# The value projection of both attention layers by the seven-product scheme

## The chip, the cores and the metric

One Trainium2 chip, one core of it. The metric is the device time of one execution in microseconds (us), the median of several runs. The program is one launch; all arithmetic is f32.

## The reference, cut to what matters

256 tokens of width 1024 pass through four layers, then through two more of another kind. Layers 0 and 3 of the first four are forgetting attention, with their own weights (j = 0 and j = 1 below):

```
h = rms_norm(x, mix_norm_g[i])
proj = h @ w_in                       # w_in 1024 x 3088
q, k, v, f_logit = split(proj, [1024, 2048, 3072])
log_f = log_sigmoid(f_logit + b_f);  c = cumsum(log_f)
p = softmax(q k^T / 8 + c_q - c_k, causal);  out = (p @ v) @ w_out
```

The change concerns `v = h @ w_in[:, 2048:3072]`, a product of 256x1024 by 1024x1024. The norm's division by the token's root mean square is a scaling of rows and is done after the product; the norm's weights are multiplied into the transposed tokens before.

## The kernel before, in words

The five engines each have one program; they meet at semaphores. Weights stream from HBM through `ring`, three slots of 128 x 6144 f32. The SyncE program issues every weight load in the order of use, three transfers per slot (line 504), each adding 16 to `loaded[slot]`; TensorE takes a slot when the count is 48 (`take`, line 1021), and gives it back with the first matmul after its last use (`release` and `carry`, lines 1048 to 1055). SyncE waits for that before it loads the slot again. For an attention layer the pieces are, in order: columns 2560 to 3087 of w_in (the right half of v and the 16 forget gates), columns 2048 to 2559 (the left half of v), four pieces of q and k, two of w_out (`fox`, line 526). The GpSimd queue loads the parameters of the S5 layer in the first microseconds (line 993), much of it in runs of 64 bytes.

The attention layer, TensorE's side (`fox`, line 1293): `raw_xT` turns the tokens, 16 transposes into banks 0 to 3; VectorE multiplies them by the norm's weights into `xT` (line 1979). Then 8 matmuls give the forget gates in bank 7 (line 1071), one matmul with a diagonal of the token scales gives these scales along columns in bank 6 (`scale_cols`, line 1129), and in layer 3 one transpose turns the norm vectors of later layers (line 1302, bank 0). The value projection is 32 matmuls of line 1082: for each half of the columns and each half of the tokens, 8 slices of the inner dimension, 128x128 by 128x512. Each bank is read by VectorE in one scaling (line 2203), into `v_rows`. After it `project(0)` (line 1316) makes the first pair of heads' q and k in bank 7, 16 matmuls; in layer 0 the transposes of `s5_inputs` follow (line 1382), and then attention, pair after pair, with `project(i + 1)` ahead of pair i.

VectorE's side (`fox`, line 2187) is one fixed order: the four xT copies, the reciprocal and diagonal of the token scales (2045, 2047), the copy of the scales (2052), forget gates (2193, 2195), in layer 3 the copy to `norm_vec` (2199), the four value scalings, the cumulative sum of the gates (2206 to 2211), in layer 0 the sign changes of S5 parameters (2263 to 2265), then the q and k scalings.

The seven-product scheme is already in use in the FFN layers: `token_sums` (line 1989) makes four sums of token blocks, `weight_sums` (2001) and `down_sums` (2015) make three new weight sums and overwrite one block, TensorE makes seven products of half the inner dimension (lines 1178 and 1230) in place of eight, and VectorE adds them up (`add_products`, line 2138). `then` (1955) has VectorE wait for its own operation before the next.

Of the kernel before, what the change touches and what calls it, by code (L numbers as in the profile page):

```python
# [10 lines left out]
S = 256  # L11
# [183 lines left out]
def build(nc, inp, table, out):  # L195
# [3 lines left out]
    with ctx:  # L199
# [87 lines left out]
        S1, S2, S3, S4 = (s_sum[:, i] for i in range(4))  # L287
        xA = [[xT[:, 4 * h:4 * h + 4, i * P:(i + 1) * P] for h in range(2)] for i in range(TT)]
# [132 lines left out]
        prods_read = sem("products_read")  # L421
        FAST_USE = [8]
# [593 lines left out]
        def _(pe):  # L1016
# [276 lines left out]
            def fox(j):  # L1293
# [658 lines left out]
        def _(dve):  # L1952
# [22 lines left out]
            def raw_xT(g, banks, sums=True):  # L1975
                for j, b in enumerate(banks):
# [5 lines left out]
                    if sums and j == 1:  # L1982
                        dve.wait_ge(drained_dve, t.value("drained_dve"))
                        token_sums(early=True)
                if sums:
                    dve.wait_ge(drained_dve, t.value("drained_dve"))
                    token_sums(early=False)

            def token_sums(early):

                (a11, a12), (a21, a22) = xA
                tt = dve.tensor_tensor
# [194 lines left out]
            def fox(j):  # L2187
                raw_xT(VEC_AT["mix_norm_g"] + 3 * j * KD, (0, 1, 2, 3), sums=False)
                scale_diag()
                full()  # L2190
                scale_cols(6)
# [4 lines left out]
                   .then_inc(dve_to_act, 1)  # L2196
                if j == 1:
# [658 lines left out]
```

## Time and profile before

| | |
|---|---|
| median of 3 runs | 2743.18 us (2739.14, 2743.18, 2746.19) |
| profiled execution, its own time | 2741.28 us |
| its span in the trace | 2739.4 us, 83867 instructions |
| TensorE matmul busy | 2651.6 us, 97% |
| TensorE weight load | 2178.2 us, 80% |
| VectorE | 1201.4 us, 44% |
| ScalarE | 356.1 us, 13% |
| mean granted TensorE clock | 0.989 of 2.4 GHz |

The profiled execution's own time is 1.9 us longer than its span; the start and the end of the launch lie around the span. Busy time of TensorE is pipelined, so 97% is not 97% of its peak. PEclk in a row of windows is the granted clock as a share of 2.4 GHz.

### The profile page before, as it was taken

To read this page: it belongs to the slowest core of one execution; us is meant where nothing else is said; L and a number is where in the kernel's file an instruction comes from. 1 tells how busy PE (TensorE), PEld (TensorE's weight loads), DVE (VectorE), ACT (ScalarE), POOL (GpSimd) and SP (SyncE) were. 2 spreads that over 40 slices of the span, in tenths; PEclk is the share of its full clock that TensorE was granted. 3 is DMA by queue.
4 is the path that set the end of the run, shared out by engine and by line. 5 is a ranking of instruction groups with operands and counts; after the bars stand their busy time and mean duration, and the time that the engine had idled before them with its cause. 6 is when DMAs were issued, how large, how long until landed. Compare 5 with 4: busy or idle time off the path is not lost.

```text
span 2739.4 us, 83867 instructions
## 1 busy us (share of the span) xinstructions
PE 2651.6 (97%) x39390; PEld 2178.2 (80%) x39390; DVE 1201.4 (44%) x1925; ACT 356.1 (13%) x730; POOL 18.5 (1%) x28
## 2 busy tenths in 40 slices
PE   8999998999999999999989999989999999999997
PEld 5789666697599466994658956559999999999996
DVE  2767864487688524885357753450000000000002
ACT  2210123100100112000240000520000101000000
POOL 1000000000000000000000000000000000000000
PEclk9999999999999999999999999989999999999999
DMA  7345422654455432545325553339999999999994
GB/s 205 123 143 167 158 74 93 208 186 170 146 162 173 176 123 90 189 148 177 121 93 170 171 185 133 108 149 386 411 410 395 393 412 393 412 394 396 410 407 186
DMA packets 269230, 619.50 MB, mean 226 GB/s; under 512 B 10326, under 2 KB 128348, under 8 KB 256636
## 3 DMA queue, kind: packets, MB, share of 16 engines
q1 hardware_dynamic: 266064, 606.14, 60.0%
q0 software_dynamic: 2400, 10.09, 1.3%
q8 instruction: 145, 2.38, 0.4%
q10 hardware_dynamic: 588, 0.63, 0.1%
q14 instruction: 33, 0.27, 0.0%
HBM read 615.77 MB, written 1.05 MB: 225 GB/s over the span
## 4 chain that ended last, share of the span: by engine, by line
PE 94%; DVE 3%; ACT 1%; issue 1%; DMA 0%; SPq 0%; DVEq 0%
PE ps L1178 25%; PE ps L1847 20%; PE ps L1862 10%; PE ps L1230 10%; PE ps L1071 8%; PE ps L1082 7%; PE ps L1266 3%; PE ps L1780 2%; PE ps L1360 2%; PE ps L1834 1%; PE ps L1814 1%; PE ps L1568 0%; PE ps L1342 0%; DMA ring<-in_fox_w_in 0%; DVE arena L2241 0%
## 5 line engine op out<-in xcount | busy, mean ns | idle before, releaser
L1847 PE MATMUL ps<-arena,ring 128*64 128x88 f32 x14336 | 550.3, 239 | 1.1 <-issue 1.1
L1847 PEld LDWEIGHTS ps<-arena,ring 128*64 128x64 f32 x14336 | 546.1, 138 | 4.9 <-issue 4.9
L2785 DVE TENSOR_TENSOR arena<-arena,ps 128x352 f32<-128x352 f32 x64 | 30.4, 476 | 728.4 <-PE ps L1847 728.4
L1071 PE MATMUL ps<-xT,ring 128*128 128x256 f32 (+2 forms) x960 | 215.0, 383 | 3.2 <-DMA ring<-in_fox_w_in 1.3
L1178 PE MATMUL ps<-arena 128*64 128x128 f32 x3520 | 211.3, 273 | 0.0
L1071 PEld LDWEIGHTS ps<-xT,ring 128*128 128x128 f32 (+2 forms) x960 | 178.5, 187 | 37.2 <-issue 7.8
L1178 PE MATMUL ps<-xT,ring 128*64 128x128 f32 x3520 | 203.9, 274 | 0.9 <-DVE xT L2549 0.9
L1178 PE MATMUL ps<-arena,ring 128*64 128x128 f32 x3520 | 201.7, 273 | 0.0
L1178 PEld LDWEIGHTS ps<-xT,ring 128*64 128x64 f32 x3520 | 195.3, 138 | 3.4 <-issue 3.1
L1178 PEld LDWEIGHTS ps<-arena 128*64 128x64 f32 x3520 | 196.4, 137 | 0.0
L1178 PEld LDWEIGHTS ps<-arena,ring 128*64 128x64 f32 x3520 | 194.3, 137 | 0.0
L1862 PE MATMUL ps<-arena,ring 128*64 128x88 f32 x4096 | 161.4, 239 | 1.0 <-issue 1.0
L1862 PEld LDWEIGHTS ps<-arena,ring 128*64 128x64 f32 x4096 | 158.0, 137 | 1.2 <-issue 1.2
L1082 PE MATMUL ps<-ring,xT 128*128 128x512 f32 (+1 forms) x320 | 131.7, 572 | 0.0
L1862 PE MATMUL ps<-arena 128*64 128x88 f32 x3072 | 122.6, 239 | 0.9 <-issue 0.9
L675 ACT ACTIVATE arena<-arena 128x512 f32<-128x512 f32 x55 | 34.7, 631 | 659.8 <-DVE arena L2117 526.0
L1862 PEld LDWEIGHTS ps<-arena 128*64 128x64 f32 x3072 | 119.2, 137 | 1.0 <-issue 1.0
L950 ACT ACTIVATE arena<-ps 128x352 f32<-128x352 f32 x64 | 27.4, 428 | 686.3 <-PE ps L1847 686.3
L1082 PEld LDWEIGHTS ps<-ring,xT 128*128 128x128 f32 x320 | 60.6, 190 | 67.7 <-issue 59.3
L1178 PE MATMUL ps<-xT,arena 128*64 128x128 f32 x1760 | 105.6, 273 | 0.0
L1178 PEld LDWEIGHTS ps<-xT,arena 128*64 128x64 f32 x1760 | 98.2, 137 | 0.0
L1230 PE MATMUL ps<-ring,arena 128*128 128x512 f32 x176 | 83.2, 595 | 0.0
(473 smaller groups left out, 2801.2 us busy)
## 6 DMA issues: line engine op xcount, KB each, us to landing
ring<-in_moe_w_gate SPq DMA_DIRECT2D x64, 1792.0 KB, 11.0
ring<-in_moe_w_up SPq DMA_DIRECT2D x64, 1792.0 KB, 11.4
ring<-in_moe_w_down SPq DMA_DIRECT2D x32, 2048.0 KB, 11.6
ring<-in_ffn_w_gate_up SPq DMA_DIRECT2D x44, 1024.0 KB, 5.2
ring<-in_ffn_w_gate_up SPq DMA_DIRECT2D x88, 512.0 KB, 7.1
arena<-in_moe_w_down SPq DMA_DIRECT2D x32, 1024.0 KB, 9.9
ring<-in_ffn_w_down SPq DMA_DIRECT2D x55, 512.0 KB, 6.0
ring<-in_ffn_w_down SPq DMA_DIRECT2D x25, 1024.0 KB, 4.9
```

The lines of the kernel that those rows point to most:

```text
L675: act.activation(gu[:, par, 0, :], gu[:, par, 0, :], ACT.Silu).then_inc(silu_ready, 1)
L950: act.activation(silu_e[:, c0 * CAP:(c0 + n) * CAP], ps[:, bank, 0:n * CAP], ACT.Silu)\
L1071: ins = pe.matmul(o, lhsT=w[:, k, c0:c0 + m], rhs=rhs[:, k, :], start=(k == 0), stop=(k == kt - 1))
L1082: ins = pe.matmul(o, lhsT=lhs[:, k0 + k, i * P:(i + 1) * P], rhs=w[:, k, c0:c0 + n], start=(k == 0), stop=(k == kt - 1))
L1178: ins = pe.matmul(o[h], lhsT=w_of[:, u, k, h], rhs=x_of[:, k, :], start=(k == 0), stop=(k == 3))
L1230: ins = carry(pe.matmul(ps[:, bank, :], lhsT=lhs, rhs=rhs[:, q, :], start=(n == 0), stop=(last and q == len(cs) - 1), skip_group_check=True))
L1266: return carry(pe.matmul(ps[:, 4 + 2 * i + half, :], lhsT=h[:, s, i], rhs=w[:, q, s, half * 512:(half + 1) * 512], start=(c == s == 0), st ...
L1360: ins = carry(pe.matmul(ps[:, b, :], lhsT=mixT[:, k, (part % 2) * P:(part % 2 + 1) * P], rhs=w[:, k, 0:512], start=(k == 0), stop=(k == 7) ...
L1780: ins = pe.matmul(ps[:, b, :], lhsT=mixT[:, k, (b % 2) * P:(b % 2 + 1) * P], rhs=w[:, k, 0:512], start=(k == 2), stop=(k == 7), skip_group ...
L1847: ins = pe.matmul(ps[h, bank, c0:c0 + CAP], lhsT=w_f[:, k, h], rhs=xe[:, 4 * kh + k, :], start=(kh == k == c0 == 0), stop=(kh == 1 and k = ...
L1862: ins = pe.matmul(o[h], lhsT=w[:, s, m * P + h.start:m * P + h.stop], rhs=hid_e[:, (s0 + s) * CAP:(s0 + s + 1) * CAP], start=False, stop=F ...
L2785: dve.tensor_tensor(hid_e[:, c0 * CAP:(c0 + n) * CAP], silu_e[:, c0 * CAP:(c0 + n) * CAP], ps[:, bank, 0:n * CAP], ALU.mult).then_inc(hid_ ...
```

## The change: the diff

In both attention layers the value projection is written as seven products of 128x512 by 512x512 in banks 0 to 6, four slices each. VectorE makes four token sums (`v_token`, in the place of `mixT`) while xT is copied, three weight sums (`v_weight`, in the place of `prob`, `probT` and `qT`), and overwrites the block b12. TensorE waits for all four token sums, makes product v4·b22, then the scale matmul, now into the second half of bank 7, and then takes the second piece. The products then follow in the order a11·b11, a12·b21, v3·t3, v1·b12, v2·t2, a22·t4, the last four each behind a weight sum. The slot of the first piece is released before v2·t2, that of the second after the last product. VectorE puts the four quarters of v together in place of the four scalings, and one count of `drained_dve`, after all of it, frees all seven banks. In layer 3 the transpose of the norm vectors comes after the products, into bank 7, and its copy after VectorE's last value operation. `FOX_USE` is the number of ring uses before each of the two layers.

```diff
@@ in build
+        v_token = arena[:, 11264:13312].rearrange("p (a k n) -> p a k n", a=4, k=4)
+        v_weight = arena[:, 2048:8192].rearrange("p (a k n) -> p a k n", a=3, n=512)
+        v_part = arena[:, 8192:9216].rearrange("p (a n) -> p a n", a=2)
+        FOX_USE = (0, 8 + 3 * FFN_USE + 7)
@@ TensorE, fox
-                holder[7] = scale_cols(6)
+                v_slots = [None, slot]
...
+                def product(bank, x_of, w_of):
+                    claim(bank)
+                    for k in range(4):
+                        ins = carry(pe.matmul(ps[:, bank, :], lhsT=x_of[:, k, :], rhs=w_of[:, k, :], start=(k == 0), stop=(k == 3)))
+                    ins.then_inc(full_dve, 1)
+                pe.wait_ge(s_ready, s0 + 4)
...
+                product(4, v4, b22)
+                pe.wait_ge(dve_to_pe, t.up("dve_to_pe"))
+                to_dve(pe.matmul(ps[:, 7, S:2 * S], lhsT=cst("ones"), rhs=r_diag[:, :, :].rearrange("p i n -> p (i n)"),
+                                 start=True, stop=True), 7)
+                v_slots[0] = take()
+                (b11, _), (b21, _) = v_blocks(v_slots)
+                product(6, a11, b11)
+                product(0, a12, b21)
+                pe.wait_ge(t_ready, sums0 + 1)
+                product(5, v3, t3)
+                pe.wait_ge(t_ready, sums0 + 2)
+                product(1, v1, b12)
+                pe.wait_ge(t_ready, sums0 + 3)
+                release(v_slots[1])
+                product(2, v2, t2)
+                pe.wait_ge(t_ready, sums0 + 4)
+                product(3, a22, t4)
+                release(v_slots[0])
+                read = (drained_dve, t.up("drained_dve"))
+                for bank in range(7):
+                    holder[bank] = read
                 if j == 1:
                     pe.wait_ge(norm_loaded, 16 * len(NORM_ROWS))
-                    claim(0)
-                    to_dve(pe.transpose(ps[:, 0, 0:NORM_TOTAL], norm_rows[:, :], ident[0:NORM_TOTAL, 0:NORM_TOTAL]), 0)
-                for i in range(TT):
-                    claim(1 + i)
-                    ins = rows(ps[:, 1 + i, :], xT, i, w, 0, 512)
-                    to_dve(ins, 1 + i)
-                release(slot)
-                slot, w = wslot(512)
-                for i in range(TT):
-                    claim(3 + i)
-                    ins = rows(ps[:, 3 + i, :], xT, i, w, 0, 512)
-                    to_dve(ins, 3 + i)
-                release(slot)
+                    claim(7)
+                    to_dve(pe.transpose(ps[:, 7, 0:NORM_TOTAL], norm_rows[:, :], ident[0:NORM_TOTAL, 0:NORM_TOTAL]), 7)
@@ VectorE, fox
+                raw_xT(VEC_AT["mix_norm_g"] + 3 * j * KD, (0, 1, 2, 3), sums=v_token)
                 scale_diag()
+                n = FOX_USE[j]
+                dve.wait_ge(loaded[n % RING], 48 * (n // RING + 1))
+                (b11, b12), (b21, b22) = v_blocks([(n + 1) % RING, n % RING])
+                t3, t2, t4 = (v_weight[:, i] for i in range(3))
+                tt(t3, b22, b12, ALU.subtract).then_inc(t_ready, 1)
                 full()
+                full()
+                full()
+                dve.wait_ge(drained_dve, drain(dve.tensor_copy(r_cols[:, :], ps[:, 7, S:2 * S])))
...
+                n += 1
+                dve.wait_ge(loaded[n % RING], 48 * (n // RING + 1))
+                then(tt(b12, b12, b11, ALU.subtract))
+                signal(t_ready)
+                then(tt(t2, b22, b12, ALU.subtract))
+                signal(t_ready)
+                tt(t4, b21, t2, ALU.subtract).then_inc(t_ready, 1)
...
+                full()
+                then(dve.tensor_copy(p2, ps[:, 6, :]))
+                full()
+                then(tt(v_at(0, 0), p2, ps[:, 0, :], ALU.add))
+                scaled(0, 0)
+                full()
+                full()
+                full()
+                then(tt(p2, p2, ps[:, 2, :], ALU.add))
+                then(tt(v_at(0, 1), p2, ps[:, 1, :], ALU.add))
+                then(tt(v_at(0, 1), v_at(0, 1), ps[:, 4, :], ALU.add))
+                scaled(0, 1)
+                then(tt(p3, p2, ps[:, 5, :], ALU.add))
+                then(tt(v_at(1, 1), p3, ps[:, 1, :], ALU.add))
+                scaled(1, 1)
+                full()
+                then(tt(v_at(1, 0), p3, ps[:, 3, :], ALU.add))
+                drain(dve.tensor_scalar(v_at(1, 0), v_at(1, 0), small[:, 7:8], None, ALU.mult))
                 if j == 1:
                     full()
-                    drain(dve.tensor_copy(norm_vec[:, :], ps[:, 0, 0:NORM_TOTAL]))
-                for c in (1, 0):
-                    for i in range(TT):
-                        full()
-                        drain(dve.tensor_scalar(v_rows[:, i, c * 512:(c + 1) * 512], ps[:, (1 if c else 3) + i, :],
-                                                small[:, 6 + i:7 + i], None, ALU.mult))
+                    drain(dve.tensor_copy(norm_vec[:, :], ps[:, 7, 0:NORM_TOTAL]))
```

## Rows read from the trace of the kernel before

**Rows 1.** The page, part 4: the chain that ended last, by engine and by line
```profile
PE 94%; DVE 3%; ACT 1%; issue 1%; DMA 0%; SPq 0%; DVEq 0%
PE ps L1178 25%; PE ps L1847 20%; PE ps L1862 10%; PE ps L1230 10%; PE ps L1071 8%; PE ps L1082 7%; PE ps L1266 3%; PE ps L1780 2%; PE ps L1360 2%; PE ps L1834 1%; PE ps L1814 1%; PE ps L1568 0%; PE ps L1342 0%; DMA ring<-in_fox_w_in 0%; DVE arena L2241 0%
```

**Rows 2.** Timeline of layer 0: start us, us, engine line op, xcount [idle before]
```profile
13.67 3.63 PE L1071 MATMUL ps<-xT,ring 128*16 128x256 f32 x16 [1.31 <-DMA ring<-in_fox_w_in]
17.23 0.70 PE L1129 MATMUL ps<-norm_scale_diagonal,const 128*128 128x256 f32 x2
17.76 27.63 PE L1082 MATMUL ps<-ring,xT 128*128 128x512 f32 x64
45.23 7.07 PE L1071 MATMUL ps<-xT,ring 128*128 128x256 f32 x32
```

**Rows 3.** Timeline of layer 3, VectorE and TensorE
```profile
947.65 2.48 DVE L1979 TENSOR_TENSOR xT<-ps,vec 128x512 f32<-128x512 f32 x4
953.22 27.68 PE L1082 MATMUL ps<-ring,xT 128*128 128x512 f32 x64
960.34 0.75 DVE L2203 TENSOR_SCALAR arena<-ps,small 128x512 f32<-128x512 f32 x1 [5.52 <-PE ps L1082]
980.74 7.07 PE L1071 MATMUL ps<-xT,ring 128*128 128x256 f32 x32
```

**Rows 4.** Line 504, third load of the second weight piece: ns, start us, landing us
```profile
L504 SPq DMA_DIRECT2D ring<-in_fox_w_in x1: 1846/1846/1846, 6.5 to 6.5; - x1
DMA to landing us min/median/max: 23.1/23.1/23.1
```

**Rows 5.** DMA view of 14 to 24 us: queue, packets, MB, share of 16 engines
```profile
DMA packets 489, 1.25 MB, mean 125 GB/s; under 512 B 48, under 2 KB 48, under 8 KB 489
q0 software_dynamic: 201, 0.69, 60.4%
```

**Rows 6.** Timeline of TensorE around two of its waits in the S5 layer
```profile
449.94 4.24 PE L1469 MATMUL ps<-arena 128*64 128x256 f32 x64 [2.38 <-DVE arena L2408]
462.06 4.11 PE L1082 MATMUL ps<-ring,arena 128*128 128x512 f32 x5 [3.18 <-ACT arena L750]
```

**Rows 7.** Windows: length, busy of PE, PEld, DVE, ACT, POOL, then PEclk, DMA share, GB/s
```profile
450.00:455.00 5.00, 4.17 (x64) 3.82 (x64) 4.79 (x10) 1.19 (x2) 0.00 (x0) 1.00 1.03 395
462.00:466.00 4.00, 3.94 (x5) 1.65 (x6) 0.00 (x0) 1.29 (x2) 0.00 (x0) 0.57 0.19 73
466.00:470.00 4.00, 4.00 (x11) 1.84 (x10) 0.00 (x0) 0.00 (x0) 0.00 (x0) 1.00 0.00 0
1749.10:1759.30 10.20, 9.89 (x60) 5.59 (x60) 5.11 (x13) 4.43 (x14) 0.00 (x0) 0.50 0.56 201
```

**Rows 8.** Line 1998, a token sum, min/median/max ns
```profile
L1998 DVE TENSOR_TENSOR arena<-xT x5: 683/692/693, 164.6 to 1457.3; 128x512 f32<-128x512 f32 x5
```

**Rows 9.** Timeline of layer 0, VectorE: the four xT copies
```profile
10.37 2.87 DVE L1979 TENSOR_TENSOR xT<-ps,vec 128x512 f32<-128x512 f32 x4 [0.63 <-PE ps L1120]
```

**Rows 10.** Line 2025, weight sums of the FFN's down part, min/median/max ns
```profile
L2025 DVE TENSOR_TENSOR arena<-ring x24: 691/1225/1226, 646.1 to 1634.5; 128x1024 f32<-128x1024 f32 x20, 128x512 f32<-128x512 f32 x4
```

**Rows 11.** Timeline of VectorE in the FFN before layer 3: two additions in a row
```profile
942.02 1.42 DVE L2068 TENSOR_TENSOR x_rows<-x_rows,arena 128x512 f32<-128x512 f32 x2
```

**Rows 12.** Line 2263, scaling 128x512 from memory to memory
```profile
L2263 DVE TENSOR_SCALAR arena<-arena x1: 426/426/426, 48.3 to 48.3; 128x512 f32<-128x512 f32 x1
```

**Rows 13.** Timeline of VectorE behind the value projection of layer 0, first and last
```profile
46.10 0.27 DVE L2206 TENSOR_SCALAR arena<-arena 16x256 f32<-16x256 f32 x1
49.07 0.43 DVE L2265 TENSOR_SCALAR arena<-arena 128x512 f32<-128x512 f32 x1
```

**Rows 14.** Line 504, the three loads issued from 45.9 to 46.8
```profile
L504 SPq DMA_DIRECT2D ring<-in_fox_w_in x3: 368/489/490, 45.9 to 46.8; - x3
DMA to landing us min/median/max: 4.5/6.1/6.9
```

**Rows 15.** Timeline of ScalarE, where the S5 parameters arrive
```profile
44.63 0.26 ACT L679 ACTIVATE arena<-arena 128x64 f32<-128x64 f32 x1 [20.05 <-DMA arena<-in_s_log_dt]
```

More of the change, by code:

```diff
@@ L287, in build, with v_blocks @@
         S1, S2, S3, S4 = (s_sum[:, i] for i in range(4))
+        v_token = arena[:, 11264:13312].rearrange("p (a k n) -> p a k n", a=4, k=4)
+        v_weight = arena[:, 2048:8192].rearrange("p (a k n) -> p a k n", a=3, n=512)
+        v_part = arena[:, 8192:9216].rearrange("p (a n) -> p a n", a=2)
+        def v_blocks(slots):
+            w = [ring[:, slot, 0:KD * n].rearrange("p (k n) -> p k n", n=n)[:, :, 0:512] for slot, n in zip(slots, (512, 528))]
+            return [[v[:, 4 * h:4 * h + 4] for v in w] for h in range(2)]
         xA = [[xT[:, 4 * h:4 * h + 4, i * P:(i + 1) * P] for h in range(2)] for i in range(TT)]
@@ L1297, in fox @@
                 to_dve(feats(ps[0:16, 7, 0:S], w, 512, 16, xT, waits=[(0, waits[1]), (4, waits[3])]), 7)
-                holder[7] = scale_cols(6)
+                v_slots = [None, slot]
+                sums0, s0 = t.count.get("t_ready", 0), t.count.get("s_ready", 0)
+                t.up("s_ready", 4)
+                t.up("t_ready", 4)
+                (a11, a12), (a21, a22) = xA
+                v1, v2, v3, v4 = (v_token[:, i] for i in range(4))
+                t3, t2, t4 = (v_weight[:, i] for i in range(3))
@@ new lines, in product @@
+                def product(bank, x_of, w_of):
[4 more added lines that the diff above has]
+                pe.wait_ge(s_ready, s0 + 4)
+                b22, b12 = (ring[:, slot, 0:KD * 528].rearrange("p (k n) -> p k n", n=528)[:, 4 * h:4 * h + 4, 0:512]
+                            for h in (1, 0))
@@ L1973, in full, with raw_xT @@
                 dve.wait_ge(full_dve, t.up("full_dve"))
-            def raw_xT(g, banks, sums=True):
+            def raw_xT(g, banks, sums=s_sum):
                 for j, b in enumerate(banks):
@@ L1981, in raw_xT, with token_sums @@
                                             vec[:, g + 4 * h:g + 4 * h + 4].unsqueeze(2).to_broadcast([P, 4, P]), ALU.mult))
-                    if sums and j == 1:
+                    if sums is not None and j == 1:
                         dve.wait_ge(drained_dve, t.value("drained_dve"))
-                        token_sums(early=True)
-                if sums:
+                        token_sums(early=True, sums=sums)
+                if sums is not None:
                     dve.wait_ge(drained_dve, t.value("drained_dve"))
-                    token_sums(early=False)
-            def token_sums(early):
+                    token_sums(early=False, sums=sums)
+            def token_sums(early, sums=s_sum):
                 (a11, a12), (a21, a22) = xA
+                S1, S2, S3, S4 = (sums[:, i] for i in range(4))
                 tt = dve.tensor_tensor
@@ L2187, in fox @@
             def fox(j):
-                raw_xT(VEC_AT["mix_norm_g"] + 3 * j * KD, (0, 1, 2, 3), sums=False)
+                tt = dve.tensor_tensor
+                raw_xT(VEC_AT["mix_norm_g"] + 3 * j * KD, (0, 1, 2, 3), sums=v_token)
                 scale_diag()
+                n = FOX_USE[j]
+                dve.wait_ge(loaded[n % RING], 48 * (n // RING + 1))
+                (b11, b12), (b21, b22) = v_blocks([(n + 1) % RING, n % RING])
+                t3, t2, t4 = (v_weight[:, i] for i in range(3))
+                tt(t3, b22, b12, ALU.subtract).then_inc(t_ready, 1)
                 full()
-                scale_cols(6)
+                full()
+                full()
+                dve.wait_ge(drained_dve, drain(dve.tensor_copy(r_cols[:, :], ps[:, 7, S:2 * S])))
                 dve.wait_ge(bias_loaded, 96)
@@ L2388, in s5 @@
                 tt = dve.tensor_tensor
-                raw_xT(VEC_AT["mix_norm_g"] + KD, (0, 1, 2, 3), sums=False)
+                raw_xT(VEC_AT["mix_norm_g"] + KD, (0, 1, 2, 3), sums=None)
                 scale_diag()
```

5 lines of the change are left out of this document (added).

## The prediction

> **What bounds the kernel now.** I read the chain that ended last first. TensorE makes 94% of it, and lines 1082 and 1071, which carry both attention projections, are in it [rows 1]. So time taken from or added to TensorE's stream shows in the end, unless a later wait swallows it. Next the timeline around each value projection. In layer 0 TensorE waits for the first weight piece until 13.67, does the 16 forget-gate instructions and the scale matmul, and then 64 value instructions without a gap from 17.76; the key/query projection follows at 45.23 [rows 2]. Layer 3 has the same block, from 953.22 to 980.74 [rows 3]. An f32 matmul shows as two instructions, so 64 are 32 matmuls. One instruction costs (45.23 - 17.76)/64 = 0.429 us, one f32 matmul 0.858 us. The new products have the same shape, 128x128 by 128x512, and take the same price.
>
> Then the loads. The second weight piece goes out in three transfers. The last of them starts to be issued at 6.5 and lands 23.1 us later [rows 4]; the two before it were down earlier, so the piece is whole at 6.5 + 23.1 = 29.6. The reason stands in the DMA view of 14 to 24: the queues are full and yet only 125 GB/s move, because the GpSimd queue (the S5 parameters, in short runs) holds 60% of the engines there [rows 5]. The old kernel asks for that piece after 32 of the 64 instructions, at 17.76 + 13.73 = 31.5: it has 2 us to spare and shows no wait. This margin is what the argument turns on.
>
> **The change, part by part.** *TensorE's arithmetic.* 28 matmuls (7 products x 4 slices) take the place of 32: 4 x 0.858 = 3.43 us less per layer, 6.87 us for both. That is the ceiling of the gain.
>
> *Order in layer 0.* The first product needs only the first piece (lower right block, with token sum v4). After it come the scale matmul and then the wait for the second piece, because a11·b11 and a12·b21 are next and both read it. Product one starts at about 17.3, where the scale matmul starts now, and ends 3.43 later at 20.7; the scale matmul adds 0.43, so TensorE asks for the second piece at 21.2. It is whole at 29.6. TensorE stands for 8.5 us, where the old order had 13.7 us of first-piece work to do. One product (v3·t3) needs the first piece alone, but the program has it behind the wait. From 29.7 the other six products are 48 x 0.429 = 20.6 us, to 50.3.
>
> *The clock.* TensorE waits 3.18 us for ScalarE at the S5 gate [rows 6], and then the granted clock averages 0.57 over 462 to 466 and is 1.00 again after that [rows 7]. (1 - 0.57) x 4 us / 0.5 = 3.4 us at 1.2 GHz instead of 2.4, a loss of 1.7 us. A wait of 8.5 us is longer than that one, so I add 1.7. The Trainium skill, "TensorE: Matmul & The Clock Gate", section "HAM oscillation — how this bites in real kernels", speaks against exactly this shape: it charges every wait for a load that lets the clock fall with half of the slow time that follows. By that rule layer 0 costs 1.7 us more than the stall; without it the sum of both layers would be +4.7 instead of +6.4. The trace agrees at this one restart and is harsher at another, which is a rival below.
>
> So the key/query projection of layer 0 starts at 50.3 + 1.7 = 52.0 instead of 45.23 (first matmul): **+6.8 us**.
>
> *VectorE in layer 0.* Four token sums at 0.69 us each (the same operation, 128x512, [rows 8]) go between and behind the xT copies, which end at 10.37 + 2.87 = 13.24 [rows 9], so the last sum ends at about 13.24 + 4 x 0.7 = 16.1; TensorE asks at 17.3: hidden behind the forget-gate matmuls, which themselves waited for a load. Weight sums are 128x2048. The rows have 128x1024 at 1.225 and 128x512 at 0.691 [rows 10]; by that slope one costs 1.225 + 1024 x 1.04 ns = 2.29 us. The first lies in the stall. The other three wait for the second piece, run 29.7 to 36.7, and are wanted by the fourth, fifth and sixth products after the restart, from about 41.7: hidden. The assembly is 8 copies and additions, 0.72 from one to the next (two of them take 1.42 [rows 11]), and 4 scalings of 0.43 [rows 12]. What follows the last product is about 2.4 us of it, under the 7 us projection, which uses bank 7 and waits for none of it. The cover is enough also for the forget-gate row sums and the S5 sign changes, 46.10 to 49.50 now [rows 13]: 52.0 + 0.3 + 2.4 + 3.4 = 58.1, while TensorE gets to the S5 transposes at 59.0. Only if that cover shrank by 1 us would this be seen.
>
> *Queues in layer 0.* The slot of the first piece is given back when the sixth product starts, at 31.4 + 4 x 3.43 = 45.1 instead of 31.5. The SyncE queue has its three transfers behind that wait. Transfers issued at 45.9 to 46.8 now land 4.5 to 6.9 us later [rows 14], so it is there by 53; the projection's key half asks at 52.0 + 3.5 = 55.5. Nothing, with 2.5 us of cover. The second slot is released at 52.0 and is asked for four head pairs later, tens of us on.
>
> *Layer 3.* Both pieces have landed long before. The xT copies start at 947.65 and take 2.48, and four sums follow inside and behind them: 947.65 + 2.48 + 4 x 0.72 = 953.0 plus 0.2 for waits, when the old value stream began at 953.22 [rows 3]. So the first product starts where the first value matmul did, the scale matmul moves behind it (0.43), and 953.25 + 3.43 + 0.43 + 20.6 = 977.7 ends the seventh product. The norm-vector transpose now goes to bank 7, and VectorE copies it out **last**. The projection claims bank 7 and so waits for that copy. VectorE sees the sixth product at 974.3 + 0.26 (now 16 instructions end at 953.22 + 6.87 = 960.08 and VectorE starts at 960.34 [rows 3]) and has three additions, a scaling, two additions, a scaling, an addition, a scaling and the 0.21 copy: 6 x 0.72 + 3 x 0.42 + 0.1 = 5.7, which gives 980.2. With 0.1 to TensorE the projection starts at 980.3 instead of 980.74: **-0.4 us**. 2.5 of the 3.4 us saved turn into a wait for VectorE. A wait of 2.38 us that ended at 449.94 left the clock at 1.00 [rows 6, 7], so I add no clock loss.
>
> **Sum.** +6.8 - 0.4 = +6.4 us, on the profiled execution's 2741.28: 2747.7. That execution lies 1.9 below the median of the three runs shown (2743.18, from 2739.14 to 2746.19). For the median I forecast **2749.6 us**, +0.23%. About 0.3%, 8.2 us, is what a measurement of this kernel can tell from no change. Bounds: the wait in layer 0 costs between nothing and 8.5 us, the clock between nothing and 5.1, layer 3 gives between 0 and 3.4.
>
> **Rivals.**
> *A: the clock stays low (slower).* From 1749.1 to 1759.3 the clock was 0.50 although TensorE was busy 9.89 of 10.2 us [rows 7]. If the restart at 29.7 is like that, the loss is 5.1 instead of 1.7: +9.8 us, 2753.0, beyond the 8.2. It decides once the slow time after the restart is longer than 3.4 + 2 x 1.8 = 7 us. For it: that row. Against: the stream behind the restart is dense 512-column work, as in 462 to 466.
> *B: the piece is there earlier (small gain).* If the second piece lands by 21.2, both layers keep what they save: -3.4 - 0.4 = -3.8, 2739.4. Nothing changes in what issues the slow transfers, so I give it little.
> *C: the stall is given back.* If a later stage of layer 0 waits anyway for something that is not moved (the S5 parameters, ready for ScalarE only at 44.63 [rows 15]), part of 6.8 us vanishes: with layer 3 about 0, 2743. Against it: TensorE does not wait there now.
> *D: no clock loss,* +4.7, 2747.9.
>
> **Chances.** Forecast 0.56, A 0.14, B 0.08, C 0.12, D 0.10. Even with both gains whole (6.87 us) the kernel would not be 0.3% faster, so "faster" has only scatter: 0.04. "Slower" takes A and the part of the forecast that scatter of a median, some 2 to 3 us, puts over 8.2: 0.14 + 0.12 = 0.26. "Same" has 0.70. The range takes in C, D, the forecast and A with a little scatter: 2742 to 2755.5; B is left out.
>
> **What the changed profile would show.** A TensorE wait of about 8.5 us on the load of the attention weights, ending near 29.6; the granted clock at half behind it for some 3.4 us; 56 instead of 64 instructions of 128x512 per layer; line 1071's first key/query matmul near 52 in layer 0; in layer 3 a wait of about 2.5 us before it that ends at VectorE's copy to norm_vec. The forecast is wrong if the wait at the second piece is under 5 us, if the six products are not 20.6 us at full clock, or if layer 0's lag at the first FFN is not the lag at its projection.

## The result and the profile after

The changed kernel takes 2755.54 us (median of seven runs, 2752.08 to 2760.86) against 2743.82 for the kernel before (seven runs, 2739.14 to 2746.19). The ratio of the comparison is 1.0051, with a 95% interval from 1.0041 to 1.0061. The kernel is slower, by 14.0 us (11.2 to 16.7). The forecast was 2749.6 with a range up to 2755.5, which the median just passes; "slower", by more than 8.2 us, had a chance of 0.26. The profiled execution took 2753.53 us, 12.3 more than the one before (2741.28). The page of the changed kernel:

```profile
span 2751.7 us, 83883 instructions
...
PE 2651.7 (96%) x39374; PEld 2178.4 (79%) x39374; DVE 1234.0 (45%) x1961; ACT 355.9 (13%) x730; POOL 18.5 (1%) x28
...
q14 instruction: 34, 0.28, 0.0%
...
PE 93%; DVE 3%; ACT 1%; DMA 1%; issue 1%; SPq 0%; DVEq 0%; ACTq 0%
...
L1080 PE MATMUL ps<-xT,ring 128*128 128x256 f32 (+2 forms) x960 | 216.6, 385 | 4.9 <-DVE norm_vec L2276 2.5
```

TensorE's busy time is the same, although it has 16 instructions of 128x512 less: what they saved (6.9 us) is spent again on instructions that run at half the clock. 2.5 and 1.8 us of that are found in the two places below; the rest is in other stretches (the mean granted clock is 0.985 instead of 0.989). In the chain [rows 1] "DMA" has gone from 0% to 1% and "PE" from 94% to 93%: a load now stands on the path.

**Layer 0.** Timeline of TensorE (start us, us, engine line operation, count [idle before]), to be read against [rows 2]:

```profile
17.45 3.70 PE L1318 MATMUL ps<-ring,arena 128*128 128x512 f32 x8
20.99 0.59 PE L1326 MATMUL ps<-norm_scale_diagonal,const 128*128 128x256 f32 x2
29.94 9.58 PE L1318 MATMUL ps<-ring,xT 128*128 128x512 f32 x16 [8.35 <-DMA ring<-in_fox_w_in]
39.35 3.60 PE L1318 MATMUL ps<-arena 128*128 128x512 f32 x8
...
53.08 7.07 PE L1080 MATMUL ps<-xT,ring 128*128 128x256 f32 x32
59.99 1.91 PE L1417 MATMUL ps<-const,arena 128*128 128x128 f32 x16
```

The load that it waits for is the third of the second piece, line 513 now (duration ns, start us; landing us), the same as in [rows 4]:

```profile
L513 SPq DMA_DIRECT2D ring<-in_fox_w_in x1: 1845/1845/1845, 6.4 to 6.4; - x1
...
DMA to landing us min/median/max: 23.5/23.5/23.5
```

6.4 + 23.5 = 29.9, and the two products go at 29.94. Behind the wait 16 instructions take 39.35 - 29.94 = 9.41 us instead of 16 x 0.429 = 6.87. The windows (length, busy of PE, PEld, DVE, ACT, POOL, then PEclk, DMA share, GB/s) say why: the granted clock, and the same again in layer 3:

```profile
28.00:30.00 2.00, 0.06 (x1) 0.07 (x1) 0.08 (x1) 0.26 (x1) 1.18 (x1) 0.50 1.05 385
30.00:35.00 5.00, 5.00 (x6) 2.12 (x7) 4.91 (x5) 0.00 (x0) 5.00 (x9) 0.51 1.11 358
35.00:40.00 5.00, 5.00 (x13) 2.28 (x12) 2.85 (x3) 0.00 (x0) 0.76 (x1) 1.00 0.99 148
988.00:990.00 2.00, 0.47 (x2) 0.47 (x3) 1.93 (x6) 0.00 (x0) 0.00 (x0) 1.00 0.04 15
990.00:994.00 4.00, 4.00 (x12) 3.21 (x12) 1.26 (x4) 0.00 (x0) 0.00 (x0) 0.58 0.68 193
994.00:998.00 4.00, 4.00 (x20) 3.50 (x19) 0.00 (x0) 0.00 (x0) 0.00 (x0) 1.00 0.91 310
```

In the first row the clock is already at 1.2 GHz before the load has landed, and it stays there for the next 5 us. Six instructions fit into these 5 us, 13 into the next.

**Layer 3.** Two rows of the kernel before that were not shown, the start of the block and its second pair of heads:

```profile
946.18 2.33 PE L1120 MATMUL ps<-const,x_rows 128*128 128x128 f32 x16
988.74 7.14 PE L1071 MATMUL ps<-xT,ring 128*128 128x256 f32 x32 [0.94 <-DVE arena L2219]
```

and the same stretch of the changed kernel:

```profile
955.28 2.33 PE L1129 MATMUL ps<-const,x_rows 128*128 128x128 f32 x16
...
986.77 0.23 PE L1348 MATMUL ps<-const,norm_rows 72*128 72x72 f32 x1
989.53 8.83 PE L1080 MATMUL ps<-xT,ring 128*128 128x256 f32 x32 [2.54 <-DVE norm_vec L2276]
999.31 7.14 PE L1080 MATMUL ps<-xT,ring 128*128 128x256 f32 x32 [0.94 <-DVE arena L2291]
```

From the transposes to the projection it is 989.53 - 955.28 = 34.25 us, where 980.74 - 946.18 = 34.56 stood: -0.3. But the projection behind the wait takes 8.83 instead of 7.07. Over the whole block, 44.03 against 42.56: +1.5.

**The end.** VectorE at the last branch of the program, before and, in the second fence, after:

```profile
2730.02 0.06 DVE L1963 MEMSET marks<- 1x1 f32 x1 [3.08 <-issue]
2730.11 0.28 DVE L2574 BATCH_NORM_AGGREGATE small<-small 128x2 f32<-128x12 f32 x2
```

```profile
2740.05 0.06 DVE L1998 MEMSET marks<- 1x1 f32 x1 [2.95 <-issue]
2742.39 0.28 DVE L2646 BATCH_NORM_AGGREGATE small<-small 128x2 f32<-128x12 f32 x2 [2.29 <-issue]
```

Both instructions belong to code that the change doesn't touch. A gap of 2.29 us has come between them. "Issue" means that no semaphore, transfer or engine explains it. Nothing else runs in parallel here, so it is in the time.

**The drift.** The same instruction in both traces, and how much later the changed kernel gets there:

| place | before | after | lag | new |
|---|---|---|---|---|
| layer 0, first key/query matmul | 45.23 | 53.08 | +7.85 | +7.85 |
| a matmul at the start of S5's scan | 126.23 | 134.09 | +7.86 | 0 |
| transposes ahead of layer 3 | 946.18 | 955.28 | +9.10 | +1.24 |
| layer 3, first key/query matmul | 980.74 | 989.53 | +8.79 | -0.31 |
| layer 3, second pair | 988.74 | 999.31 | +10.57 | +1.78 |
| a later layer | 1402.73 | 1415.09 | +12.36 | +1.79 |
| the layer behind it | 1771.17 | 1780.61 | +9.44 | -2.92 |
| last matmuls | 2720.42 | 2730.57 | +10.15 | +0.71 |
| the span | 2739.4 | 2751.7 | +12.3 | +2.15 |

Three places make most of it: layer 0 +7.85, the block in layer 3 +1.5, the end +2.2. The other steps, +1.24, +1.79, -2.92 and +0.71, add up to +0.8.

The +1.24 comes from two waits of TensorE that the kernel before has too, and in code that the change doesn't touch. Here is the first of them before, then both after; the second is to be read against 449.94 in [rows 6]:

```profile
126.23 0.88 PE L1568 MATMUL ps<-const,arena 128*128 128x128 f32 x6 [3.07 <-DVE arena L2253]
```

```profile
134.09 1.54 PE L1603 MATMUL ps<-const,arena 128*128 128x128 f32 x6 [3.08 <-DVE arena L2325]
458.47 5.74 PE L1504 MATMUL ps<-arena 128*64 128x256 f32 x64 [2.42 <-DVE arena L2480]
```

The waits are as long as before. Yet the work behind them takes 1.54 us instead of 0.88 and 5.74 instead of 4.24, and the granted clock of the 2 us behind the first is 0.50 instead of 1.00. The lag is +8.53 at the second wait and +9.09 at the S5 gate behind it (471.15 against 462.06), and so it is the whole +1.24.

The last three, +1.79, -2.92 and +0.71, are put down to stretches at half clock that come in one execution and not in the other, in code that is the same: the one at 1749.1 [rows 7] is much shorter after.

### The profile page after: what moved, and what is told of

Read it like the earlier page. It is cut to its first block, busy times and chain, and to the rows that moved or that the text cites. A ratio compares the mean times of both kernels' runs of the same rounds, so it can differ in the third digit from the quotient of the medians.

```text
span 2751.7 us, 83883 instructions
## 1 busy us (share of the span) xinstructions
PE 2651.7 (96%) x39374; PEld 2178.4 (79%) x39374; DVE 1234.0 (45%) x1961; ACT 355.9 (13%) x730; POOL 18.5 (1%) x28
## 4 chain that ended last, share of the span: by engine, by line
PE 93%; DVE 3%; ACT 1%; DMA 1%; issue 1%; SPq 0%; DVEq 0%; ACTq 0%
PE ps L1187 25%; PE ps L1882 20%; PE ps L1897 10%; PE ps L1239 10%; PE ps L1080 8%; PE ps L1091 5%; PE ps L1275 3%; PE ps L1395 2%; PE ps L1815 2%; PE ps L1318 2%; PE ps L1869 1%; PE ps L1849 1%; DMA ring<-in_fox_w_in 1%; PE ps L1504 1%; PE ps L1603 0%
## 5 line engine op out<-in xcount | busy, mean ns | idle before, releaser
L1239 PE MATMUL ps<-arena,ring 128*128 128x512 f32 x176 | 82.7, 592 | 0.0
L1239 PE MATMUL ps<-ring 128*128 128x512 f32 x176 | 79.4, 592 | 0.0
## 6 DMA issues: line engine op xcount, KB each, us to landing
ring<-in_moe_w_down SPq DMA_DIRECT2D x32, 2048.0 KB, 11.6
```

The source lines that it names most:

```text
L1239: ins = carry(pe.matmul(ps[:, bank, :], lhsT=lhs, rhs=rhs[:, q, :], start=(n == 0), stop=(last and q == len(cs) - 1), skip_group_check=True))
```

## The experiments

Every kernel was compared with the kernel before, run beside it on the same chip: e1 to e4 on one, e5 to e8 on a second, e9 to e11 on a third. The table gives, for all of them, the three places read from their profiles, their sum, and what the comparison measured (ratio less one, times the median of the kernel before). S5 is the start of the S5 transposes in layer 0, behind the first projection (52.14 before). Block is the time from layer 3's transposes to its second pair (42.56 before). End is the gap at the last branch (none before).

| kernel | S5 | block | end | sum | measured us, 95% |
|---|---|---|---|---|---|
| changed | 59.99 | 44.03 | 2.29 | +11.6 | +14.0, 11.2 to 16.7 |
| e1 | 52.01 | 44.01 | 0 | +1.3 | +3.0, 0.5 to 5.5 |
| e2 | 56.94 | 44.02 | 2.54 | +8.8 | +9.9, 6.3 to 13.4 |
| e3 | 51.43 | 44.02 | 2.29 | +3.0 | +8.5, 5.5 to 11.8 |
| e4 | 59.36 | 39.60 | 2.27 | +6.5 | +6.6, 4.1 to 9.1 |
| e5 | 59.34 | 44.01 | 0 | +8.7 | +10.7, 6.9 to 14.3 |
| e6 | 52.37 | 42.57 | 0 | +0.2 | 0.0, -2.5 to 2.7 |
| e7 | 55.38 | 43.98 | 0 | +4.7 | +6.9, 4.1 to 9.3 |
| e8 | 50.12 | 39.61 | 0 | -5.0 | -4.1, -6.6 to -1.6 |
| e9 | 52.55 | 39.60 | 0 | -2.6 | -4.1, -6.6 to -1.6 |
| e10 | 52.24 | 42.57 | 0 | +0.1 | +0.3, -2.2 to 2.7 |
| e11 | 48.64 | 39.61 | 0 | -6.5 | -4.4, -6.9 to -1.9 |

Eleven of twelve sums lie in their interval. The exception is e3. But the sums are not all of it: the eight kernels with the seven products in layer 0 all measured above their sum, by 0.1 to 5.5 us. A fourth place accounts for part of that, the stretch from the S5 transposes to layer 3, 894.04 us before. All ten kernels with seven products in either layer are slower there, by 1.3 to 4.3 us (changed 1.3, e1 1.3, e2 2.9, e3 4.3, e4 1.3, e5 3.6, e7 3.7, e8 3.7, e9 2.1, e11 1.5); e6 and e10, without them, by 0.0 and 0.1. The two waits shown above tell the same: 3.07 to 3.08 and 2.37 to 2.43 us long in all thirteen profiles, each followed within 4 us by a fallen clock in the ten (5.73 to 5.90 us for the instructions behind the second) and by none in the three (4.24). So this is not mere scatter, nor does the length of the wait alone decide. What in the change decides it no run shows: in e1, layer 0 takes what it took before, and the clock falls at 126 all the same.

### e1: the change in layer 3 alone

```diff
-                product(4, v4, b22)
+                if j == 1:
+                    product(4, v4, b22)
...
+                else:
+                    for i in range(TT):
...
```

> Edit: the seven products in layer 3 alone; layer 0 has its old 32 matmuls. If layer 0's wait for the second weight piece carries the loss (theory), this kernel has no wait over 1 us in front of the value projection of layer 0 and stands within 3 us of the kernel before: layer 3 gives back 0.3 to 0.4 us, and the wait of 2.5 us for the norm_vec copy may lower the clock for 3.4 us, 1.8 us of loss. Expected ratio 1.0000 to 1.0008. Rival (the form itself costs, in layer 3 as much as in layer 0): +5 us or more, ratio over 1.0018.

2745.39 us (2740.93 to 2751.38), ratio 1.0011 [1.0002, 1.0020]. Layer 0 is as before, with the S5 transposes at 52.01 (52.14 before). Its layer 3 on TensorE:

```profile
981.56 8.83 PE L1080 MATMUL ps<-xT,ring 128*128 128x256 f32 x32 [2.54 <-DVE norm_vec L2295]
```

The same 2.54 and 8.83 as in the changed kernel. So what layer 3 does is its own and not a consequence of layer 0: the seven products save 3.4 us there and the block is still 1.5 longer. Of the change's +14.0 at most 5.5 belong to layer 3. The rest is not in this kernel: what layer 0 costs, and the 2.3 at the end.

### e2: the wait of layer 0 filled with matmuls

Nine matmuls of 128x512 are added ahead of the wait, into a bank that is overwritten.

```diff
+                if j == 0:
+                    claim(6)
+                    for f in range(9):
+                        pe.matmul(ps[:, 6, :], lhsT=v4[:, f % 4, :], rhs=b22[:, f % 4, :], start=True, stop=True)
                 v_slots[0] = take()
```

> Edit: changed kernel, with nine 128x512 matmuls (7.7 us) put into the wait of layer 0; their result is overwritten by the product that uses the bank. If the clock falls because of the wait (theory), the products after the wait run at 0.43 us an instruction from the first on, and layer 0's projection starts 2.5 us earlier than in the changed kernel, near 50.5. Median 2 to 3.5 us below the changed kernel's. Rival (the wait alone is the loss, the clock comes and goes by itself): no difference.

2751.72 us (2750.73 to 2756.98), ratio 1.0036 [1.0023, 1.0049]. TensorE, and in the second fence the window:

```profile
21.00 7.89 PE L1331 MATMUL ps<-ring,arena 128*128 128x512 f32 x18
29.33 7.13 PE L1318 MATMUL ps<-ring,xT 128*128 128x512 f32 x16 [0.45 <-DMA ring<-in_fox_w_in]
36.30 3.60 PE L1318 MATMUL ps<-arena 128*128 128x512 f32 x8
```

```profile
30.00:35.00 5.00, 5.00 (x13) 2.14 (x12) 4.92 (x5) 0.00 (x0) 5.00 (x8) 1.00 1.12 332
```

TensorE does useless work for as long as it stood, and the kernel's block is 3.05 us shorter. Of these, 9.41 - 6.97 = 2.4 us are the clock (the first two products, 29.33 to 36.30, against 29.94 to 39.35). 0.6 us is the load, which landed that much sooner in this execution. By the medians the kernel is 3.8 us below the changed one, a little more than the 2 to 3.5 expected. The rival without any clock loss is out. So is the one with 5.1 us: the slow time behind the restart is one of 5 us, not of 10. The Trainium skill ("TensorE: Matmul & The Clock Gate", section "HAM oscillation — how this bites in real kernels") has the cost as half of the slow time. Here 5 us at half clock cost 2.4 to 2.5: the trace agrees with the rule, and the duration that I had put in was too short.

### e3: GpSimd's loads behind the second piece

GpSimd's queue waits until the second piece is down, then issues seven loads (output maps, rates and steps), then the four input maps of S5, which now have a semaphore of their own.

```diff
+            pool.wait_ge(loaded[1], 48)
-            for dst, src in loads:
+            for dst, src in loads[4:]:
...
+            for dst, src in loads[:4]:
+                pool.dma_start(dst, src, allow_slow_non_contiguous=True).then_inc(s5_b_loaded, 16)
```

> Edit: changed kernel, but the GpSimd queue starts its loads of S5 parameters when the second weight piece has landed, the output maps, rates and steps first and the input maps last, which VectorE awaits by a semaphore of their own just before it reads them. If those loads hold the second piece back (theory), it lands near 19 to 20, before TensorE asks at 21.2; no wait, full clock; the projection of layer 0 starts at 41.8 to 42 (before: 45.23, changed: 53.08). Whole kernel 11 us below the changed one, 2 to 4 below the kernel before. Rival (the weight queue is slow for itself): the piece lands near 29 as before, no gain. A second danger: the later loads are now awaited themselves, seen as a wait for c_in or s5 parameters near 48.

2752.16 us (2747.05 to 2756.11), ratio 1.0031 [1.0020, 1.0043]. TensorE, then GpSimd:

```profile
21.04 7.03 PE L1322 MATMUL ps<-ring,xT 128*128 128x512 f32 x16
...
41.64 3.62 PE L1084 MATMUL ps<-xT,ring 128*128 128x256 f32 x16
47.87 3.72 PE L1084 MATMUL ps<-xT,ring 128*128 128x256 f32 x16 [2.61 <-DMA ring<-in_fox_w_in]
```

```profile
19.40 1.04 POOL L1004 DMA_DIRECT2D arena<-in_s_c_re  x1 [18.95 <-DMA ring<-in_fox_w_in]
```

The second piece is down by 19.4 instead of 29.9, and the 8.35 us wait is gone: the mechanism of the stall is shown. The amount of weights is the same; what held them back were GpSimd's transfers. That these are slow for themselves can be seen here: in e3 they are nearly alone in the queues from 26 to 36 and move 82 GB/s, with the engines busy for 78% of the time, where the weights alone move 387 GB/s from 9 to 19. That the reason is their runs of 64 bytes is likely, but no experiment changes those.

Part of the gain comes back as a new wait, the second danger of the expectation. The input maps now go out from 24.0 on, and the first slot's reload, wanted at 45, runs beside them. That is the place from which e8 and e11 start. So the median is 3.4 us below the changed kernel's instead of the 11 expected, and above the kernel before instead of below it. The sum of the three places explains 3.0 of the 8.5 us. In the profile TensorE has lost another 4.3 us between S5's transposes and layer 3 (949.77 there, 3.6 later than before, after having been 0.7 ahead). They lie where the clock fell: the lag is -0.70 at the first of the two waits named under the table (125.53), +1.48 at the second (451.42), +2.19 at the S5 gate behind it (464.25), +3.21 at 700 us of the old time and +3.59 at layer 3. From 460 to 470 the mean clock is 0.66 instead of 0.83. With the 4.3 the sum is 7.3 and inside the interval. e5 and e7, which leave the loads alone, have 3.6 and 3.7 of the same, so it isn't the loads.

### e4: the norm-vector copy early

```diff
                 product(4, v4, b22)
...
+                if j == 1:
+                    pe.wait_ge(norm_loaded, 16 * len(NORM_ROWS))
+                    claim(5)
+                    to_dve(pe.transpose(ps[:, 5, 0:NORM_TOTAL], norm_rows[:, :], ident[0:NORM_TOTAL, 0:NORM_TOTAL]), 5)
                 v_slots[0] = take()
...
-                    claim(7)
-                    to_dve(pe.transpose(ps[:, 7, 0:NORM_TOTAL], norm_rows[:, :], ident[0:NORM_TOTAL, 0:NORM_TOTAL]), 7)
```

VectorE copies it before the product that uses bank 5 comes round.

> Edit: changed kernel, but the norm-vector transpose of layer 3 goes to bank 5 behind the scale matmul and VectorE copies it before the weight sums. Theory: the 2.54 us wait before layer 3's key/query projection is gone, and with it the clock's fall behind it; the step from the first xT transpose of layer 3 to the first key/query matmul is 2.5 us shorter than in the changed kernel (34.25 there), and 1.8 us more come back where the clock had fallen. Median 2.5 to 4.5 us below the changed kernel. Rival (VectorE's assembly is awaited by something else right after): the wait reappears at the first scores and the gain is under 1 us.

2749.31 us (2747.75 to 2750.63), ratio 1.0024 [1.0015, 1.0033]. Layer 3 on TensorE:

```profile
954.74 2.33 PE L1129 MATMUL ps<-const,x_rows 128*128 128x128 f32 x16
...
986.33 7.07 PE L1080 MATMUL ps<-xT,ring 128*128 128x256 f32 x32
994.34 7.14 PE L1080 MATMUL ps<-xT,ring 128*128 128x256 f32 x32 [0.94 <-DVE arena L2291]
```

No wait and no half clock: the block takes 39.60 us, 4.43 less than in the changed kernel, and 2.96 less than before. That is 2.7 of wait and 1.76 of clock, all for one copy of 0.23 us that stood last in VectorE's order. Most of a layer's 3.43 us was there and lay behind it. By the medians the kernel is 6.2 us below the changed one, more than the 2.5 to 4.5 expected and more than this place gives. The projection at 8.83 occurs in all six profiles with this wait (changed, e1, e2, e3, e5, e7) and in none of the seven without it.

### e5 and e6: longer code on VectorE

24 memsets of one element into a spare tile stand at the start of VectorE's program (e5, in the changed kernel), or 45 of them (e6, in the kernel before, about as many instructions as the change adds).

```diff
+            for i in range(24):
+                dve.memset(spare[:, i:i + 1], 0.0)
```

> Edit: changed kernel with 24 one-element memsets of a spare tensor at the start of VectorE's program, where it waits for the constants. Theory: the 2.3 us in which VectorE stands between its first and its second instruction behind the last branch (2740.05 to 2742.39 in the changed kernel, waiting for nothing in the profile) come from where that place falls in its instruction memory; 24 instructions later the gap is gone, and the median is 2 to 2.5 us below the changed kernel's. Rival (the gap belongs to something that is computed): it stays, and 24 more instructions change nothing.

> Edit: the kernel before with 45 such memsets, about as many instructions as the change adds to VectorE's program. Theory (place of the code): a gap of 2.3 us appears behind the last branch in a kernel that computes just what the kernel before does, ratio 1.0008. Rival: no gap, ratio 1.0000. If 45 misses the place by a few instructions the gap does not show either; then only the run with 24 more speaks.

e5: 2753.36 us (2751.97 to 2756.78), ratio 1.0039 [1.0025, 1.0052]. e6: 2742.47 (2738.89 to 2744.64), ratio 1.0000 [0.9991, 1.0010]. VectorE in e5:

```profile
2745.54 0.06 DVE L1999 MEMSET marks<- 1x1 f32 x1 [3.02 <-issue]
2745.64 0.28 DVE L2649 BATCH_NORM_AGGREGATE small<-small 128x2 f32<-128x12 f32 x2
```

The gap has gone although instructions were *added*, so it is not work. The page has something beside it: queue 14, kind "instruction", moved 33 packets of 8 KB in the kernel before and 34 in the changed one, and 33 again here. In all kernels the gap and a 34th (in e4 a 35th) packet come together: changed, e2, e3 and e4 have both, the other nine neither. That extra loading of code goes with the gap is an inference from this count.

That the place of the code decides it is not shown. e6 did not call the gap forth in the kernel before. And e7, whose VectorE program has the changed kernel's instructions, no more and no fewer, has no gap either. So 24 more instructions are not needed to lose it, and what made it vanish in e7 may have done so in e5 too. Every kernel has one profile, so that a gap which comes and goes from execution to execution of one kernel isn't ruled out, nor one that hangs on the chip (e2, e3 and e4, which have it, ran on the chip of e1, which hasn't; none of e5 to e11 has it on the other two). The medians don't settle it: e5 is 2.2 us below the changed kernel, as expected, but the intervals of the two overlap.

### e7: the product v3·t3 ahead of the wait

```diff
                 product(4, v4, b22)
...
+                pe.wait_ge(t_ready, sums0 + 1)
+                product(5, v3, t3)
                 v_slots[0] = take()
                 product(6, a11, b11)
                 product(0, a12, b21)
-                pe.wait_ge(t_ready, sums0 + 1)
-                product(5, v3, t3)
```

> Edit: changed kernel with the product v3 t3, which needs the first piece alone, before the wait for the second piece (in both layers). Theory: the wait of layer 0 shrinks from 8.35 to 4.9 us (24.5 to 29.4), five products follow instead of six, and the key/query projection starts near 47 at full clock, 48.7 if the clock still falls: 4.4 to 6 us earlier than in the changed kernel. Median 4 to 6 us below it. Rival (the landing moves with TensorE's use of the piece, or the wait is for VectorE's sums): the projection stays near 53.

2749.84 us (2743.97 to 2755.98), ratio 1.0025 [1.0015, 1.0034]. TensorE:

```profile
21.04 3.60 PE L1318 MATMUL ps<-arena 128*128 128x512 f32 x8
29.51 8.83 PE L1318 MATMUL ps<-ring,xT 128*128 128x512 f32 x16 [4.87 <-DMA ring<-in_fox_w_in]
```

3.43 us of work fit into the stall, as they should, and layer 0 is 4.6 us shorter. Yet a wait of 4.87 still lets the clock fall, for 1.8 us, and the layer is 3.2 behind the kernel before. By the medians the kernel is 5.7 us below the changed one, as expected, but reordering the products alone doesn't save it: only two of the seven live on the first piece, and after them TensorE is at 24.6, five us ahead of the load.

### e8 and e11: all three mended; e9: layer 3 alone, mended

e8 is e3's loads, with the input maps issued only when the first slot is loaded again (`pool.wait_ge(loaded[0], 96)`), e4's copy and e5's memsets. e11 differs in one line from e8, and lets the maps wait for the second slot instead:

```diff
-            pool.wait_ge(loaded[0], 96)
+            pool.wait_ge(loaded[1], 96)
```

e9 is e1 with e4's copy.

> Edit: changed kernel with four edits: S5 output maps, rates and steps loaded from the second weight piece on, S5 input maps only after the fifth piece load (the first slot's second load) has landed; norm-vector copy early in layer 3; 24 memsets at the start of VectorE's program. Theory: no wait over 1 us for a weight piece in layer 0, projection's second half not held back (it was by 2.61 us with the loads of the run before), s5 transposes at 48.8 against 52.14 in the kernel before; layer 3 3.1 us shorter than before; no gap behind the last branch. Sum -3.4 - 3.1 = -6.5 us, median near 2737, ratio 0.9976, plus or minus 0.001 by the clock. Rival (the savings are taken back by clock falls or by the later loads of the S5 maps): ratio 0.999 to 1.001, and the profile shows a wait for the S5 maps or more half-clock stretches than before.

> Edit: the seven products in layer 3 alone, with the norm-vector copy early; layer 0 as in the kernel before. Theory: nothing but layer 3's own saving of 3.0 to 3.1 us, first xT transpose to second key/query projection 39.6 us against 42.56, no half clock near 980. VectorE's program grows by some 22 instructions, as in the run with layer 3 alone, which had no gap behind the last branch. Median 2739.5 to 2740, ratio 0.999. Rival: the clock takes it back elsewhere, ratio 1.000.

> Edit: mended kernel with the S5 input maps loaded later still, after the second slot's second load. In the mended run VectorE's sign changes of 128x512 took 1.56 and 1.61 us instead of 0.43 while the GpSimd queue issued those loads, and TensorE waited 1.12 us for them. Theory (the two engines get in each other's way): with the issues moved the sign changes take 0.43 again, the wait of 1.12 us is gone, S5 transposes at 48.9 against 50.1, and the median is about 1 us lower, 2737.5 to 2738. Rival: the slow sign changes have another cause and stay.

e8: 2738.81 us (2736.42 to 2741.89), ratio 0.9985 [0.9976, 0.9994]. e9: 2738.85 (2737.51 to 2741.73), ratio 0.9985 [0.9976, 0.9994]. e11: **2737.44** (2734.45 to 2740.60), ratio 0.9984 [0.9975, 0.9993], the lowest of all kernels run. VectorE in layer 0 of e8:

```profile
46.87 1.56 DVE L2342 TENSOR_SCALAR arena<-arena 128x512 f32<-128x512 f32 x1
48.46 1.61 DVE L2343 TENSOR_SCALAR arena<-arena 128x512 f32<-128x512 f32 x1
```

TensorE in e8:

```profile
50.12 1.97 PE L1423 MATMUL ps<-const,arena 128*128 128x128 f32 x16 [1.12 <-DVE arena L2343]
```

GpSimd in e8 at the same time:

```profile
44.77 1.65 POOL L1009 DMA_DIRECT2D arena<-in_s_b_re  x1 [20.53 <-DMA ring<-in_fox_w_in]
46.40 3.42 POOL L1009 DMA_DIRECT2D arena<-in_s_b_im  x2
```

And e11, TensorE and then VectorE:

```profile
41.73 7.07 PE L1086 MATMUL ps<-xT,ring 128*128 128x256 f32 x32
48.64 1.91 PE L1423 MATMUL ps<-const,arena 128*128 128x128 f32 x16
```

```profile
46.65 0.42 DVE L2342 TENSOR_SCALAR arena<-arena 128x512 f32<-128x512 f32 x1
47.10 0.43 DVE L2343 TENSOR_SCALAR arena<-arena 128x512 f32<-128x512 f32 x1
```

In e8 two of the three sign changes of 0.43 us take 1.6 while GpSimd issues its loads, and S5's transposes wait for the last: they start at 50.12 instead of the 48.8 expected. In e11 GpSimd issues from 50.34 on and both are gone. Layer 0 then gives 52.14 - 48.64 = 3.5 us and layer 3 2.95: both gains of the seven products, nearly whole (3.43 each is TensorE's arithmetic). The intervals of e8, e9 and e11 overlap, so that e11 is faster than e9 is read from the profiles and not shown by the times. Against the changed kernel the gain of e11 is 18 us.

### e10: the kernel before with its loads reordered

```diff
+            pool.wait_ge(loaded[1], 48)
...
+            pool.wait_ge(loaded[0], 96)
```

> Edit: the kernel before with the S5 loads moved as in the mended kernel (maps, rates and steps from the second piece on, input maps after the first slot's second load). It tells whether the mended kernel's gain is the products' or the loads'. Theory: the kernel before never waited for the second piece, so nothing is gained: value projection from 17.7 to 45.1, key/query projection at 45.1 to 45.3, ratio 0.9995 to 1.0005. Rival: the loads themselves cost it time, ratio below 0.999.

2742.20 us (2739.80 to 2745.38), ratio 1.0001 [0.9992, 1.0010]. The order of the loads is worth nothing by itself. It pays only where the products want the second piece early.

## Why the prediction was right or wrong

- **The stall in layer 0: right.** Forecast: asks at 21.2, whole at 29.6, 8.5 us. Measured: 21.6, 29.9, 8.35. e3 shows that the crowded queues are its cause: with GpSimd's loads out of the way the piece is there by 19.4.
- **"a loss of 1.7 us" of clock in layer 0: this term was too small.** It cost 2.4 to 2.5 us. I took the price from a wait of 3.18 us. The clock was already down when the load landed, and it then ran at half for the first 5 us of work instead of 3.4. That makes 53.08 instead of 52.0 with the 0.3 us of the later landing.
- **"A wait of 2.38 us that ended at 449.94 left the clock at 1.00 …, so I add no clock loss": this step failed.** A wait of 2.54 us cost 1.76 us in six profiles of six. I had a row on either side, 2.38 without loss and 3.18 with, and took the side of the nearer one as certain instead of keeping 1.7 as the other end. Nor was the row a rule. The very same wait, 2.42 us long at 458.47 in the changed kernel, did lower the clock (5.74 us of work instead of 4.24), as it did in all ten kernels with the products; and the trace of before held a longer one, 3.07 us ahead of 126.23, without a loss. So neither the loss nor its absence can be read from the length of one wait. The wait itself was forecast to 0.04 us, its place and its releaser too, and "-0.4" was -0.3. With the clock, layer 3 gives +1.5 instead of -0.4.
- **The end: not in the sum at all.** 2.2 us at the last branch come from no operation of the change. The gap goes with one more packet of code loaded; e7 has VectorE's same instructions and no gap, so its cause stays open. I had counted instructions on engines and transfers in queues, but nothing for this.
- **The sum.** 7.85 - 6.8 = 1.0, 1.5 + 0.4 = 1.9, 2.2 and 0.8 of other stretches (with +1.24 at two old waits in it) are 5.9: forecast +6.4, profile +12.3. The likeliest case had the direction and the place of more than half of it.
- **The rivals.** A (clock low for 10 us) is not what happened: 5 us were slow. B (piece there in time, small gain) is what e3, e8 and e11 bring about by hand. That its sum, -3.8, is close to e11's measured -4.4 is luck: e11 also has the early copy, which B hasn't, and its own places add up to -6.5. C (stall given back): out, the lag is 7.85 at the projection and 7.86 at 126 us of the old time. D (no clock loss): out by e2.
- **VectorE: right.** A weight sum took 2.29 us as worked out from the slope of two shapes, and the sign changes ended at 58.9, before TensorE wanted them at 59.99:

```profile
29.92 2.29 DVE L2243 TENSOR_TENSOR ring<-ring 128x2048 f32<-128x2048 f32 x1 [6.95 <-DMA ring<-in_fox_w_in]
...
58.45 0.43 DVE L2337 TENSOR_SCALAR arena<-arena 128x512 f32<-128x512 f32 x1
```

- **The reloads in layer 0: right**, no wait in the changed kernel. e3, with a wait of 2.61 us there, shows how little it takes to change that.
- **The range** ended at 2755.5. It held the clock at its worst in layer 0, but nothing for the clock in layer 3, for the end and for the old waits.

## What to carry to other kernels

A scheme with fewer products wants its inputs sooner. Compare the time at which each is asked for with its landing in the trace, not with the bytes: loads in another queue can hold it back by 10 us, as here. Then look at what stands last in VectorE's order and holds a bank: one copy of 0.23 us cost 4.4. Price a new wait of TensorE like the ones here (2.5, 4.9 and 8.4 us) with a clock loss of 1.7 to 2.5 us on top, and don't take an old wait of 2.4 or 3.1 us for free because it was free once: here the same wait cost clock in ten kernels and none in three.

## What the runs showed of the hardware that was not expected

- **VectorE slowed by GpSimd.** A 128x512 f32 scaling from memory to memory takes 0.43 us, and 1.56 and 1.61 us while GpSimd issues loads (e8, against 0.42 and 0.43 in e11). The Trainium skill ("SBUF — State Buffer", section "Who interferes with whom") says that the two engines share one pair of ports, that some VectorE operations, scalings among them, take it, and that whichever comes first blocks the other. The rows agree in part: the two slow scalings run while GpSimd issues from 46.40 to 49.82, and none is slow in e11, where it issues nothing then. But a scaling at 46.53 in e8 took 0.43 all the same.
- **The same wait, two prices.** Waits of 3.08 and 2.4 us that all thirteen profiles have are followed by a fallen clock in ten of them and by none in three (see under the table); why is open.
- **A gap behind a branch.** 2.3 to 2.5 us in four of thirteen profiles, each time with one or two more packets of code loaded. What brings it stays open.
- **Times scatter with the clock.** Over the 76 runs of the kernel before beside e1 to e11, from 2737.5 us at a mean granted clock of 0.989 to 2748.5 at 0.982. Stretches at half clock (in the kernel before one of 10 us, [rows 7], and one that holds all of 1825 to 1840) come and go in code that is the same, so differences under 3 us between two profiles are read place by place, and not from their spans.
